# Matmuls of constants into an unread bank during the five waits for a norm

## The reference

```
for layer in range(2):                                # first_block
    h = hybrid_mixer(x, ...)                          # projections, attention, delta rule, convolution, w_o
    x = layer_norm(ALPHA * x + h, ln1_g, ln1_b)       # norm 0, norm 2
    f = swiglu(x, w1, w3, w2) if layer == 0 else moe_swiglu(x, router_w, ...)   # 8 experts, top 2
    x = layer_norm(ALPHA * x + f, ln2_g, ln2_b)       # norm 1, norm 3
# second block
y = rms_norm_2(x, norm1_g)                            # follows norm 3 at once
x = x + (block_attention(...) | rg_lru(...)) @ w_out
y = rms_norm_2(x, norm2_g)                            # ahead of the last feed-forward
x = x + conv_gated_ffn(y, w_up, w_down)
out = rms_norm_2(x, final_g)
```

## Time and profile before

| | |
|---|---|
| median of three runs | 2310.25 us (2308.36 to 2311.13) |
| profiled execution, its own time | 2302.45 us |
| span from first to last instruction | 2300.6 us |
| mean granted TensorE clock (1.00 is 2.4 GHz, 0.50 is 1.2 GHz) | 0.969 |
| TensorE busy with matmuls | 2156.1 us, 94% of the span |
| VectorE, ScalarE, GpSimd busy | 1392.5, 1108.7, 1180.7 us |

### The profile page before, as it was taken

The page is one execution under the profiler, slowest core; times in us unless marked ns, Lnnn a source line. Parts: engine busy times, 40 slices in busy tenths (PEclk is TensorE's granted clock), DMA queues, the critical chain, the costliest instruction groups (busy, mean ns, idle before and its releaser), DMA issues.

```text
span 2300.6 us, 26818 instructions
## 1 busy us (share of the span) xinstructions
PE 2156.1 (94%) x10612; PEld 1729.5 (75%) x10612; DVE 1392.5 (61%) x1801; ACT 1108.7 (48%) x1111; POOL 1180.7 (51%) x465
## 2 busy tenths in 40 slices
PE   8999899989997899999999999999999996998997
PEld 7577588875685677777777777888777775758997
DVE  4565633365656577777777775443467777535665
ACT  1232243312331576767677674433367674444553
POOL 0120055401200698989899895555479894103543
PEclk9999899999998999999999999999999998989999
DMA  8200454522004698989999896555579896315560
GB/s 307 73 1 28 162 205 174 201 98 74 1 3 162 230 361 327 364 314 362 347 329 358 313 359 250 183 183 183 183 262 359 317 361 218 111 37 201 184 220 19
DMA packets 208095, 484.41 MB, mean 211 GB/s; under 512 B 9169, under 2 KB 13009, under 8 KB 207057
## 3 DMA queue, kind: packets, MB, share of 16 engines
q1 hardware_dynamic: 207952, 482.50, 57.8%
HBM read 481.44 MB, written 1.05 MB: 210 GB/s over the span
## 4 chain that ended last, share of the span: by engine, by line
PE 87%; DVE 7%; ACT 3%; issue 2%; POOL 1%; DMA 0%; DVEq 0%; ACTq 0%; SPq 0%; POOLq 0%
PE bank L957 21%; PE bank L959 20%; PE bank L958 20%; PE bank L594 12%; PE bank L786 5%; PE bank L601 3%; PE bank L747 1%; DVE b_arena L1338 1%; DVE b_X L1338 1%; ACT e_hi L2210 1%; PE bank L703 1%; PE bank L864 1%; PE bank L1221 1%; POOL e_lo L2759 1%; DVE b_arena L1344 1%
## 5 line engine op out<-in xcount | busy, mean ns | idle before, releaser
L2759 POOL TENSOR_TENSOR e_lo<-b_ring,e_hi 128x512 fp32r<-128x512 f32 (+1 forms) x401 | 1122.7, 2821 | 636.3 <-ACT e_hi L2210 636.3
L1810 DVE TENSOR_TENSOR e_lo<-b_ring,e_hi 128x1536 fp32r<-128x1536 f32 (+2 forms) x407 | 782.0, 1922 | 480.6 <-ACT e_hi L2210 479.3
L2210 ACT ACTIVATE e_hi<-b_ring 128x2048 fp32r<-128x2048 f32 (+1 forms) x407 | 777.2, 1912 | 336.5 <-PE bank L959 330.5
L957 PE MATMUL bank<-e_hi,e_xh 128*128 128x512 f32 (+1 forms) x1200 | 476.6, 397 | 33.6 <-issue 15.7
L959 PE MATMUL bank<-e_hi,e_xl 128*128 128x512 f32 (+1 forms) x1200 | 467.3, 389 | 0.0
L958 PE MATMUL bank<-e_lo,e_xh 128*128 128x512 f32 (+1 forms) x1200 | 467.0, 389 | 0.0
L957 PEld LDWEIGHTS bank<-e_hi,e_xh 128*128 128x128 f32 x1200 | 227.1, 189 | 100.4 <-issue 52.6
L957 PE MATMUL bank<-e_hi,e_th 128*128 128x512 f32 x688 | 272.4, 396 | 0.7
L958 PE MATMUL bank<-e_lo,e_th 128*128 128x512 f32 x688 | 268.5, 390 | 0.0
L959 PE MATMUL bank<-e_hi,e_tl 128*128 128x512 f32 x688 | 268.3, 390 | 0.0
L959 PEld LDWEIGHTS bank<-e_hi,e_xl 128*128 128x128 f32 x1200 | 226.9, 189 | 48.2
(11 more groups left out here) (234 smaller groups left out, 2316.0 us busy)
## 6 DMA issues: line engine op xcount, KB each, us to landing
b_ring<-in_moe_w SPq DMA_DIRECT2D x168, 2048.0 KB, 8.1
b_ring<-in_w_in SPq DMA_DIRECT2D x15, 2048.0 KB, 8.7
b_ring<-in_ffn_w SPq DMA_DIRECT2D x15, 2048.0 KB, 7.8
b_ring<-in_w_up SPq DMA_DIRECT2D x12, 2048.0 KB, 7.8
b_ring<-in_w_down SPq DMA_DIRECT2D x6, 2048.0 KB, 8.7
b_ring<-in_w_o SPq DMA_DIRECT2D x4, 2048.0 KB, 7.7
b_gain<-in_gains SPq DMA_DIRECT2D x6, 1024.0 KB, 4.8
b_ring<-in_w_out SPq DMA_DIRECT2D x2, 2048.0 KB, 8.3
```

Of the source, the lines that this page charges most:

```text
L957: e.matmul(out, ah, bh, start=first, stop=False)
L1810: e.tensor_tensor(lo[:, 0:at], raw[:, 0:at], r32(hi[:, 0:at]), ALU.subtract).then_inc(lo_dve.sem)
L2210: return e.activation(out, x, ACT.Copy)
L2759: e.tensor_tensor(lo[:, at:], raw[:, at:], r32(hi[:, at:]), ALU.subtract).then_inc(lo_pool.sem)
```

## The change

A helper `keep_up(n, b)` issues n matmuls. Each multiplies the identity by the first 512 columns of the constants tile `cst` (identity, ones, the constant 1/256, a triangle), all float32, and writes the 128 x 512 result over bank b. No instruction waits for them, they wait for nothing and signal nothing. They are called at the five places listed above, in front of the transposes, with n = 6, 10, 6, 16 and 5; b is a bank whose earlier content is no longer needed and that the next stage starts afresh. There are 43 such matmuls. No other engine's program changes.

```diff
@@ in pe(e) @@
+            def keep_up(n, b):
+
+                for _ in range(n):
+                    e.matmul(bank[b][:, :], ident, cst[:, 0:512], start=True, stop=True)
@@ in pe(e), the list of stages @@
             turn_rows(X, 0, lambda t, h: [])
             mixer(0)
+            keep_up(6, 0)
             turn_split(X, 0, lambda t, h: [ln_out(0, t + 2 * h)])
             gated(FF0_UNITS, FF0_P, 0, 2)
+            keep_up(10, 0)
             turn_rows(X, 1, lambda t, h: [ln_out(1, t + 2 * h)])
             mixer(1)
+            keep_up(6, 0)
             turn_rows(X, 2, lambda t, h: [ln_out(2, t + 2 * h)])
             router()
             experts()
+            keep_up(16, 0)
             turn_rows(HN, 3, lambda t, h: [rms_out(0, 2 * t + h)])
             third()
+            keep_up(5, 7)
             last_feed()
```

## The result

The changed kernel takes 2299.61 us (median of 20 runs, 2292.32 to 2305.39); the kernel before, run beside it, 2307.06 us (20 runs, 2303.0 to 2311.13). The ratio is 0.9969, with a 95% interval of 0.9961 to 0.9977: 7.2 us faster, 5.3 to 9.0. I had forecast 2.4 us faster. The time also lies just under the low end of the range, 2300.5. Part of that is the base: with more runs the kernel before has a median of 2307.06, not the 2310.25 from which I had started.

What follows compares the result with a forecast made beforehand. TensorE was taken to bound the kernel, with transposes at norms waiting for VectorE. The terms summed to -2.4 us, taken from the median 2310.25 to give 2307.8 us; range 2300.5 to 2313.0.

Steps and rivals of the forecast that it cites:

- the sum: Adding the parts at norms 0 to 4: -0.1 - 0.4 - 0.3 - 1.9 + 0.3 = -2.4 us.
- term for norm 3: At norm 3, faster transposes and product save 3.15 us in all; six tenths, 1.9 us, was taken.
- term for norm 4: At norm 4, transposes save 0.3 us, against a one-in-three clock fall costing 1.7 us; +0.3 us taken.
- What bounds the kernel: TensorE bounds the kernel, busy 2156.1 of 2300.6 us; at norms its transposes wait for VectorE and its clock may drop.
- the cost of the constants: At all five norms the constants fit their waits at the high clock, 0.4 to 0.9 us left; cost taken as 0.
- Does the clock hold: Behind the constants the clock falls amid the transposes at norms 0, 1 and 2, but mostly holds at norm 3.
- The row that I had leaned on: At norm 3, one gap of 2.38 us between dense products was enough for the clock to be 0.50.
- The terms 1.05 and 2.1: At norm 3 with the clock held: transposes end 1.05 us earlier and the product behind them saves 2.1 us.
- -0.1, -0.4 and -0.3 were taken: Savings in us taken at norms 0, 1 and 2; upper bounds 2.6, 0.84 and 0.84.
- the clock holds everywhere: Rival: the high clock holds at all five norms, saving 7.7 us, thus 2302.5 us; chance 0.20.

Runs made afterwards that it cites:

- two_each: The changed kernel with two constant matmuls at each of the five norms instead of 6, 10, 6, 16 and 5; ratio 0.9988 to the kernel before.
- double: The changed kernel with all five numbers doubled to 12, 20, 12, 32 and 10; ratio 1.0046 to the kernel before, 10.6 us slower.
- fill: The changed kernel plus two constants between first and second transpose groups (norms 0, 1, 2) and two behind the last (norms 0, 4); ratios 0.9947, 0.9965.
- before_again: The kernel before, unchanged, profiled a second time; the text gives no separate time or ratio for it.
- attention_fed: The changed kernel plus one constant matmul in each of five steps of the last attention; ratio 0.995 to the kernel before.

## Why the prediction was wrong

The step that failed is the sum. Its term for norm 3 (-1.9) was too small, its term for norm 4 (+0.3) had the wrong sign, and it had no term for other stages. The runs show -3.2 and -0.7 in place of the first two; what other stages give stays open.

**What bounds the kernel, and the cost of the constants: right.** All five bursts ran at 1.00 and fitted; 5.31, 8.75, 5.31, 13.90 and 4.46 us in the profile. two_each shows that they work by reaching up to the transposes, and double that they cost by overrunning.

**Does the clock hold: right at norms 0, 2 and 3.** At norms 0 and 2 it fell before or amid the transposes in all four profiles of the changed kernel, at norm 1 in three of them. At norm 3 it held in all four. fill shows the reason by the other side: with the 2 us between the first and second group (and at norm 0 the wait for the remainders) filled, it held through the transposes at norms 0 to 2 as well. The row that I had leaned on, 0.50 behind a gap of 2.38 us, shows what can happen and not what must: behind the same gap the clock held in nine of the twenty profiles. The Trainium skill's rule of short idle gaps ("TensorE: Matmul & The Clock Gate", HAM oscillation) would have had it hold: the gaps left behind the constants at norm 0 were 1.00, 2.00 and 1.41 us. The trace disagrees, and decides.

**Norm 3 was sized too small.** The terms 1.05 and 2.1 were right (-3.1 in the first two profiles), but I took six tenths of them, for fear that the clock might fall or that other executions of before lose less. It fell in one of nine. The mean of the four profiles of the changed kernel is -3.5, of the ten without sixteen constants there -0.25: a gain of 3.2 us, not 1.9. (Both means hold the 0.7 us of luck from the adding back.)

**Norm 4 had the wrong sign.** I took +0.3, from -0.3 for the transposes and a one-in-three fall of the clock in the 2 us behind them. The clock held there in every profile with five or more constants. The remainders on VectorE, which I believed to be the bound, had themselves been held up by the slow transposes: they now take 2.48 us instead of 3.18, -0.7 each time.

**Norms 0 and 1: sizes right, within their scatter; norm 2 gave nothing.** -0.1, -0.4 and -0.3 were taken; the means of four profiles against those without constants at the place are -0.1 (-1.2 against -1.1), -0.5 (+0.5 against +1.1 over eight) and 0, without scatter.

**What the forecast left out: other stages.** Against -2.4, norms 3 and 4 account for -3.2 - 0.7 = -3.9, norm 1 perhaps for -0.5. The router, which has no constants, was 2 us or more later than in the first profile of before in six of the eleven profiles of kernels without the full five sets, and in one of the nine with them (means +1.8, and +0.7 over the four of the changed kernel). If that is an effect, it is -1.1, and the sum, with norm 0's -0.1, is -5.6, within the measured 5.3 to 9.0. It is not shown. The same means differ by -2.1 in "rest" (-1.4 against +0.75), and by -1.7 in "ahead" (-0.35 against +1.3), where no kernel differs: chance alone moves such a mean by that much. The slow form of this stage looks thus in before_again:

```profile
732.80:739.40 6.60, 1.15 (x5) 0.75 (x5) 5.88 (x17) 2.43 (x4) 0.00 (x0) 0.50 0.00 0
739.50:763.30 23.80, 17.72 (x81) 17.19 (x82) 8.91 (x33) 3.28 (x5) 1.80 (x1) 0.50 0.81 308
```

The clock does not come back in the transposes, and the gathers and the first expert start at 0.50. So 3.9 us of the 7.2 are assigned, to norms 3 and 4. The other 3.3, of which norm 1, the router and "rest" may each hold some, stay open. The rival "the clock holds everywhere" named 7.7 us, close to the measured figure, and its mechanism is nevertheless false: at norms 0 and 2 the clock fell every time. A matching total proves nothing about the parts.

**The range** was too narrow at the low end because I took one execution's places of the low clock as fixed and allowed 2 us for them; 20 runs of before span 8.1 us.

## What to carry to other kernels

Fill an engine's wait in front of dense work only if the filling reaches up to that work and the short pieces between are dense too; ask for each gap behind the filling what lies in it. Where the clock depends on what ran before, compare profiles stage by stage, record against record, and take several of each kernel before reading a difference of a few microseconds. A term's discount for chance should come from counted executions: norm 3's was taken at six tenths, and the clock held there in eight of nine profiles.

## What the runs showed that was not expected

The clock's pattern isn't the same from one execution to the next. The product behind norm 0 lost the 2.4 us in three of six profiles with six constants there, and in five of ten without.

One dense float32 matmul (0.85 us) in each thin step of the attention, with head steps of 3.67 us (2020.47 to 2024.14 from one constant to the next in attention_fed), is cheaper than the same step at 0.50, 5.07 us (2022.14 to 2027.21 in the first profile of before). What let the clock fall is not settled. TensorE had idled for 0.64 us (to 2019.50) shortly before the clock fell at 2021.6, and in attention_fed this idle time is gone too. What the rows show is that TensorE, busy for 20.13 of 20.30 us with the thin products, stayed at 0.50.
